# Both attentions of the first block: probabilities as the moving operand, division by the sums moved to GpSimd

## The chip, the cores and the metric

The kernel runs on one core of one Trainium2 chip. The metric is the device time of one execution in microseconds (us), the median of three runs. TensorE is called PE, VectorE DVE, ScalarE ACT, GpSimd POOL.

## The reference, cut to what matters

The program is two transformer blocks. The change lies in the first, which has two layers (`l` = 0, 1) over 256 positions of width 1024. Each layer has a mixer with two self attentions of 8 query heads (2 key and value heads of 64), then a cross attention of 4 heads of 128 to a memory of 256 rows:

```python
p = jax.nn.softmax(jnp.concatenate([s, sink_l], axis=-1), axis=-1)[..., :-1]   # window attention
o = jnp.einsum('bnkgqs,bnskd->bnqkgd', p.astype(v.dtype), vw)
p = jax.nn.softmax(s, axis=-1)                                                 # dense attention
return jnp.einsum('bkgqs,bskd->bqkgd', p.astype(v.dtype), v)
s = jnp.einsum('bqhd,bmhd->bhqm', q, k).astype(jnp.float32) / math.sqrt(X_HEAD_DIM)
p = jax.nn.softmax(s, axis=-1)                                                 # cross attention
o = jnp.einsum('bhqm,bmhd->bqhd', p.astype(v.dtype), v)
return o.reshape(B, S, X_WIDTH) @ wo
```

The division by the softmax sums can be done on the probabilities or on the output; the result is the same.

## The kernel before, in words

**Weights.** Every large product is done as three products of rounded halves. A weight arrives by DMA in pieces of up to 128x1024 elements (`raw`), ACT rounds it (`wh`, L1047), and DVE subtracts to get the rest (`lows`, L1579, two SBUF inputs). PE then runs `three`: high by high, high by low, low by high (L492, in the helper `run`). `lows_for` and `highs_of` look ahead by `LA = 3` pieces: when DVE comes to item n of its program, it makes the low part of piece n + 3.

**Self attention.** The 16 heads are worked on in 8 units of 4 heads and 128 queries (`unit(un)`; `hold` is the place of the unit in S and PT, which alternates). Between the steps of the units stand the `fills`, which are products that don't depend on them: 24 gate products (one 128x1024 piece each), then 24 branch products (`merge`, 128x512 each). Iteration `un` on PE is: the scores of unit `un` (L704), the transposes of the exponentials of unit `un - 1` (`probs_turned`, in L602), three fills, `finish(un - 1)`: the product with the values (L683), one more fill, and the transposes of the output (`oT`, in L602). After iteration 7 the transposes and `finish` of unit 7 follow. There are two layers, so 16 units. DVE takes the maxima of a unit, waits for ACT's exponentials (`sums`), takes the reciprocal of the sums (L1816), makes the lows of the fills, multiplies the product with the values by that reciprocal (`o`, L1841), and after ACT has copied the high half of the transposed output (`oh`, L1179) takes the low half (`ol`, L1845). In the merge fills DVE also has a multiply by the gate for each (`mul`, L1768).

**Cross attention.** Scores (L760); exponentials; the value projection `mv` of four pieces; 16 transposes of the exponentials (L602); 16 products with the values (L778); `xo` on DVE (L1919), 8 transposes of the output, the halves `xoh` (L1249) and `xol` (L1924), and the output projection `wo`, whose four pieces each need their low part (L1579).

**PSUM banks.** The small products rotate over the four banks of `A`. `A.take(w, name, *until)` takes the next bank and waits for the `until` of what was in it four takes before. Each engine's order is that of the program text; each `w.wait_ge` blocks all that stands behind it on that engine.

## Time and profile before

| | before |
|---|---|
| median of 3 runs | 1575.55 us (1572.67 to 1577.36) |
| the profiled execution, its own time | 1578.58 us |
| its span from first to last instruction | 1576.8 us |
| PE busy | 1527.9 us (97%) |
| DVE busy | 1034.4 us (66%) |
| ACT busy | 792.9 us (50%) |
| POOL busy | 228.5 us (14%) |

The span is 1.8 us less than the execution's own time. A busy PE is not a PE at its peak, since matmul records overlap; what a group of matmuls costs is the distance from its first start to the start of what follows. An fp32 matmul stands in the records twice, an fp32 transpose once.

### The profile page before, as it was taken

To read this page: it belongs to the slowest core of one execution; us is meant where nothing else is said; L and a number is where in the kernel's file an instruction comes from. 1 tells how busy PE (TensorE), PEld (TensorE's weight loads), DVE (VectorE), ACT (ScalarE), POOL (GpSimd) and SP (SyncE) were. 2 spreads that over 40 slices of the span, in tenths; PEclk is the share of its full clock that TensorE was granted. 3 is DMA by queue.
4 is the path that set the end of the run, shared out by engine and by line. 5 is a ranking of instruction groups with operands and counts; after the bars stand their busy time and mean duration, and the time that the engine had idled before them with its cause. 6 is when DMAs were issued, how large, how long until landed. Compare 5 with 4: busy or idle time off the path is not lost.

```text
span 1576.8 us, 24954 instructions
## 1 busy us (share of the span) xinstructions
PE 1527.9 (97%) x10255; PEld 1378.4 (87%) x10255; DVE 1034.4 (66%) x1704; ACT 792.9 (50%) x1373; POOL 228.5 (14%) x190
## 2 busy tenths in 40 slices
PE   9999999899999999999999999999999999999999
PEld 6899989799987889988879998687998899989887
DVE  5765586778856585468578874746584687666743
ACT  5554453466643446444546663344445764455532
POOL 2300032121101130021121110103010132100000
PEclk9989999999999999999999999999998999999999
DMA  8623255355565534245444555555311344645453
GB/s 315 244 97 109 92 209 194 117 203 180 183 218 176 198 116 152 70 138 201 181 160 166 185 198 187 192 187 204 118 58 62 108 147 146 209 165 183 169 191 121
DMA packets 40353, 258.19 MB, mean 164 GB/s; under 512 B 4512, under 2 KB 5168, under 8 KB 14000
## 3 DMA queue, kind: packets, MB, share of 16 engines
q1 hardware_dynamic: 35600, 238.44, 43.4%
q0 software_dynamic: 2272, 12.57, 2.2%
q10 hardware_dynamic: 2368, 5.58, 0.9%
q8 instruction: 81, 1.33, 0.3%
q14 instruction: 32, 0.26, 0.1%
HBM read 254.98 MB, written 1.07 MB: 162 GB/s over the span
## 4 chain that ended last, share of the span: by engine, by line
PE 79%; DVE 11%; ACT 6%; DMA 2%; issue 1%; POOL 1%; ACTq 0%; POOLq 0%; DVEq 0%; SPq 0%
PE ps L492 68%; DVE lows L1579 5%; PE ps L602 4%; ACT wh L1047 3%; PE ps L683 2%; PE ps L968 1%; DMA raw<-d_wst 1%; PE ps L704 1%; PE ps L981 1%; ACT arR L1560 1%; DVE S L2306 1%; DVE xTr L1598 1%; PE ps L722 1%; PE ps L778 0%; PE ps L721 0%
## 5 line engine op out<-in xcount | busy, mean ns | idle before, releaser
L1579 DVE TENSOR_TENSOR lows<-raw,wh 128x1024 fp32r<-128x1024 f32 (+3 forms) x473 | 545.0, 1171 | 249.0 <-ACT wh L1047 246.4
L492 PE MATMUL ps<-xTr,wh 128*128 128x256 f32 (+2 forms) x3472 | 635.5, 285 | 6.7 <-DVE lows L1579 4.6
L492 PEld LDWEIGHTS ps<-xTr,wh 128*128 128x128 f32 (+2 forms) x3472 | 539.5, 191 | 11.7 <-ACT arR L1498 3.6
L1047 ACT CAST wh<-raw 128x1024 fp32r<-128x1024 f32 (+3 forms) x473 | 455.0, 989 | 170.4 <-DMA raw<-d_wst 127.8
L492 PE MATMUL ps<-xTr,lows 128*128 128x256 f32 (+1 forms) x1736 | 492.1, 283 | 0.0
L492 PEld LDWEIGHTS ps<-xTr,lows 128*128 128x128 f32 (+1 forms) x1736 | 330.9, 191 | 0.0
L492 PE MATMUL ps<-wh,arR 128*128 128x512 f32 x928 | 297.9, 398 | 7.4 <-DVE ar L1768 4.0
L492 PEld LDWEIGHTS ps<-wh,arR 128*128 128x128 f32 x928 | 175.2, 189 | 52.3 <-DVE ar L1768 5.7
L492 PE MATMUL ps<-lows,arR 128*128 128x512 f32 x464 | 183.9, 396 | 0.0
L492 PE MATMUL ps<-wh,xTr 128*128 128x512 f32 x480 | 152.5, 395 | 16.2 <-DVE xTr L1598 13.2
L492 PE MATMUL ps<-arR,wh 128*128 128x256 f32 (+1 forms) x832 | 148.0, 280 | 0.3
L492 PEld LDWEIGHTS ps<-arR,wh 128*128 128x128 f32 (+1 forms) x832 | 126.7, 188 | 1.1 <-issue 0.8
L492 PEld LDWEIGHTS ps<-wh,xTr 128*128 128x128 f32 x480 | 90.8, 189 | 39.0 <-DVE xTr L1598 15.2
L492 PE MATMUL ps<-arR,lows 128*128 128x256 f32 (+1 forms) x416 | 115.9, 279 | 0.0
L492 PEld LDWEIGHTS ps<-lows,arR 128*128 128x128 f32 x464 | 87.7, 189 | 20.0
L2323 POOL TENSOR_TENSOR sm<-sm,cst 128x1 f32<-128x1 f32 (+3 forms) x27 | 43.2, 1602 | 392.5 <-DVE sm L1618 255.5
L492 PE MATMUL ps<-lows,xTr 128*128 128x512 f32 x240 | 94.0, 392 | 0.0
L492 PEld LDWEIGHTS ps<-arR,lows 128*128 128x128 f32 (+1 forms) x416 | 78.1, 188 | 0.0
L1294 ACT ACTIVATE S<-ps,ar 128x256 f32<-128x256 f32 x88 | 48.6, 561 | 46.1 <-PE ps L492 46.0
L2387 POOL TENSOR_TENSOR ar<-ar 128x256 f32<-128x256 f32 x32 | 31.9, 997 | 233.8 <-DVE ar L1768 233.8
L2399 POOL TENSOR_TENSOR S<-S 128x256 f32<-128x256 f32 x44 | 34.3, 779 | 208.4 <-ACT S L1273 208.4
L492 PEld LDWEIGHTS ps<-lows,xTr 128*128 128x128 f32 x240 | 45.5, 190 | 9.1
(259 smaller groups left out, 1501.7 us busy)
## 6 DMA issues: line engine op xcount, KB each, us to landing
raw<-d_wst SPq DMA_DIRECT2D x196, 1024.0 KB, 4.8
raw<-d_wst SPq DMA_DIRECT2D x24, 512.0 KB, 3.5
raw<-d_wst SPq DMA_DIRECT2D x12, 896.0 KB, 4.5
raw<-d_wst SPq DMA_DIRECT2D x8, 672.0 KB, 4.6
ar<-d_lnp POOLq DMA_DIRECT2D x5, 1024.0 KB, 5.1
raw<-d_wst SPq DMA_DIRECT2D x8, 441.0 KB, 3.4
ar<-d_par POOLq DMA_DIRECT2D x2, 1192.0 KB, 9.6
ar<-d_scr POOLq DMA_DIRECT2D x1, 2048.0 KB, 8.6
```

The source lines that it names most:

```text
L492: op = e.matmul(out, s, m, start=start and i == 0, stop=stop and i == len(pairs) - 1)
L602: op = e.transpose(o, x, ident[0:x.shape[0], 0:x.shape[0]])
L683: op = e.matmul(b[:, h * 64:(h + 1) * 64], PTv[:, hold + h, k, :], va[:, k, v:v + 64], start=(k == 0), stop=(k == 1))
L704: op = e.matmul(bv[:, k, :], qT[br][lo:lo + 64, 2 * hh + k, i * 128:(i + 1) * 128], kT[br][lo:lo + 64, :], start=True, stop=True)
L722: op = e.matmul(bv[:, gg, :], ones[:, 0:128], bs[:, gg * 128:(gg + 1) * 128], start=False, stop=True)
L968: op = e.matmul(b[:, h * 65:(h + 1) * 65], PTv[:, hold + h, k, :], vb[:, k, 4 * br + h, :], start=(k == 0), stop=(k == nkt - 1))
L1047: e.copy(high_of(m), raw_of(m)).then_inc(*high.done(m))
L1294: e.activation(hc[:, s, :], M["up", l, m][:, 0:T], ACT.Identity, bias=cb[:, m:m + 1], scale=ck[:, m, 1:2]).then_inc(*act.done("h", l, m))
L1579: e.tensor_tensor(low_of(m), raw_of(m), high_of(m).bitcast(F32), ALU.subtract).then_inc(*low.done(m))
L2323: return e.tensor_tensor(dst, src, mhalf[0:p, 0:n], ALU.pow)
L2387: e.tensor_tensor(merged[:, d, :], merged[:, d, :], gates[:, gate_at[n] + d, :], ALU.add).then_inc(*pool.done("merged", l, n, d))
L2399: e.tensor_tensor(hc[:, s, :], hc[:, s, :], hc[:, s + 1, :], ALU.mult).then_inc(*pool.done("z", l, n))
```

## The change

In both attentions the operands of the product with the values change places. The values become the stationary operand and the transposed probabilities move, so that the output comes out transposed and the output's transposes on PE, their banks and the buffers `osb`, `xo` go. In the self attention two heads that share their values are now one matmul of 64 output rows and 256 columns, and the two value heads write the rows 0 to 63 and 64 to 127 of one bank. A multiply by the reciprocal on the output is no longer possible in this form, so POOL scales the exponentials in place, 128x1024 elements a unit, between `sums` and the transposes. ACT and DVE take the halves straight from the product's bank, which is given back at `ol`.

```diff
                 def probs_turned(un):
                     hold = unit(un)[3]
-                    w.wait_ge(act, "exp", l, un, 3)
+                    w.wait_ge(pool, "probs", l, un)
...
                 def finish(un):
                     br, i, hh, hold = unit(un)
-                    b = A.take(w, ("pv", l, un), vec, "o", l, un)
+                    b = A.take(w, ("pv", l, un), vec, "ol", l, un)
+                    bv = b[:, 0:256].rearrange("p (h q) -> p h q", q=128)
...
-                    for h in range(4):
-                        v = 128 * br + (h % 2) * 64
-                        for k in range(2):
-                            op = e.matmul(b[:, h * 64:(h + 1) * 64], PTv[:, hold + h, k, :], va[:, k, v:v + 64],
+                    for k in range(2):
+                        for g in range(2):
+                            v = 128 * br + g * 64
+                            op = e.matmul(bv[64 * g:64 * g + 64, :, :], va[:, k, v:v + 64], PTv[:, hold + g:hold + g + 3:2, k, :],
                                           start=(k == 0), stop=(k == 1))
                     op.then_inc(*cross.done("pv", l, un))
                     fill_next(1)
-                    b = A.take(w, ("oT", l, un), vec, "ol", l, un)
-                    bv = b[:, 0:256].rearrange("p (k t) -> p k t", t=128)
-                    w.wait_ge(vec, "o", l, un)
-                    turned(("oT", l, un), [bv[:, k, :] for k in range(2)],
-                           [osb[:, 64 * hold + k * 128:64 * hold + (k + 1) * 128] for k in range(2)])
...
-                    w.wait_ge(act, "xexp", l, i, 3)
+                    w.wait_ge(pool, "xprobs", l, i)
...
-                            op = e.matmul(b[:, h * 128:(h + 1) * 128], PTv[:, 4 * i + h, k, :], Vx[:, k, h * 128:(h + 1) * 128],
+                            op = e.matmul(b[:, h * 128:(h + 1) * 128], Vx[:, k, h * 128:(h + 1) * 128], PTv[:, 4 * i + h, k, :],
...
-                for i in range(2):
-                    b = A.take(w, ("xoT", l, i), vec, "xol", l, i)
-                    bv = b[:, :].rearrange("p (k t) -> p k t", t=128)
-                    w.wait_ge(vec, "xo", l, i)
-                    turned(("xoT", l, i), [bv[:, k, :] for k in range(4)], [xo[i][:, k * 128:(k + 1) * 128] for k in range(4)])
...
-                    w.wait_ge(cross, "pv", l, un)
-                    w.wait_ge(vec, "ri", l, un)
...
-                    e.tensor_tensor(osb[:, 64 * hold:64 * hold + 256].rearrange("p (h d) -> p h d", d=64),
-                                    A["pv", l, un][:, 0:256].rearrange("p (h d) -> p h d", d=64),
-                                    ri.unsqueeze(2).to_broadcast([128, 4, 64]), ALU.mult).then_inc(*vec.done("o", l, un))
...
+                def probs_scaled(un):
+
+                    hold = unit(un)[3]
+                    ri = smalls(96 + 48 * (un % 2))[3]
+                    w.wait_ge(vec, "ri", l, un)
+                    e.tensor_tensor(Sv[:, hold:hold + 4, :], Sv[:, hold:hold + 4, :], ri.unsqueeze(2).to_broadcast([128, 4, T]),
+                                    ALU.mult).then_inc(*pool.done("probs", l, un))
+
+                probs_scaled(0)
                 w.wait_ge(vec, "qg", l, 1)
                 rope_sin(1, 1)
+                for un in range(1, 8):
+                    probs_scaled(un)
...
+                for i in range(2):
+                    ri = smalls(96 + 48 * i)[3]
+                    w.wait_ge(vec, "xri", l, i)
+                    e.tensor_tensor(Sv[:, 4 * i:4 * i + 4, :], Sv[:, 4 * i:4 * i + 4, :], ri.unsqueeze(2).to_broadcast([128, 4, T]),
+                                    ALU.mult).then_inc(*pool.done("xprobs", l, i))
```

Three places in the engines' queues. First PE, at the end of iteration 1 of layer 0: the output's transposes (`ps<-cst,ar`), the scores of unit 2 (`ps<-ar`), and the transposes of unit 1's exponentials (`ps<-cst,S`). Before:

```order
L602 MATMUL ps<-cst,ar 128x128 [waits s_vec]
L602 MATMUL ps<-cst,ar 128x128
L704 MATMUL ps<-ar 128x256 x4
L602 MATMUL ps<-cst,S 128x128 [waits s_act]
L602 MATMUL ps<-cst,S 128x128 x3
L602 MATMUL ps<-cst,S 128x128 [waits s_vec]
L602 MATMUL ps<-cst,S 128x128 x3
```

And of the changed kernel:

```order
L699 MATMUL ps<-ar 128x256 [waits s_vec]
L699 MATMUL ps<-ar 128x256 x3
L601 MATMUL ps<-cst,S 128x128 [waits s_pool]
L601 MATMUL ps<-cst,S 128x128 x3
L601 MATMUL ps<-cst,S 128x128 [waits s_vec]
L601 MATMUL ps<-cst,S 128x128 x3
```

The two transposes with their wait for DVE are gone, and the first group of transposes of the exponentials waits for POOL where it waited for ACT. The second group waits for DVE in both: it takes the bank that `ol` of the unit before gives back.

Second DVE, in iteration 1: the reciprocal, the four lows of the fills, `o` and `ol`, and the copy of the transposed exponentials. Before:

```order
L1816 RECIPROCAL sm<-sm 128x4 [waits s_vec]
L1579 TENSOR_TENSOR lows<-raw,wh 128x1024 [waits s_high] x4
L1841 TENSOR_TENSOR ar<-ps,sm 128x256 [waits s_cross]
L1845 TENSOR_TENSOR arR<-ps,arR 128x2x128 [waits s_act]
L1827 COPY PT<-ps 128x512 [waits s_cross]
```

And of the changed kernel:

```order
L1806 RECIPROCAL sm<-sm 128x4 [waits s_vec]
L1569 TENSOR_TENSOR lows<-raw,wh 128x1024 [waits s_high] x4
L1825 TENSOR_TENSOR arR<-ps,arR 128x2x128 [waits s_act]
L1817 COPY PT<-ps 128x512 [waits s_cross]
L1782 ISA S,sm<-ps,cst 128x256
```

Only `o` is gone; the four lows still follow the reciprocal that POOL's new operation waits for.

Third POOL in layer 0. Before:

```order
L2380 TENSOR_TENSOR ar<-ar 128x512 [waits s_pool]
L2357 TENSOR_TENSOR ar<-ar,cst 128x10x32 [waits s_vec]
L2387 TENSOR_TENSOR ar<-ar 128x256 [waits s_vec] x8
L2387 TENSOR_TENSOR ar<-ar 128x256 [waits s_pool,s_vec] x8
L2323 TENSOR_TENSOR sm<-sm,cst 128x1 [waits s_vec] x2
```

And of the changed kernel:

```order
L2353 TENSOR_TENSOR ar<-ar 128x512 [waits s_pool]
L2360 TENSOR_TENSOR S<-S,sm 128x1024 [waits s_vec]
L2330 TENSOR_TENSOR ar<-ar,cst 128x10x32 [waits s_vec]
L2360 TENSOR_TENSOR S<-S,sm 128x1024 [waits s_vec] x7
L2372 TENSOR_TENSOR ar<-ar 128x256 [waits s_vec] x8
L2372 TENSOR_TENSOR ar<-ar 128x256 [waits s_pool,s_vec] x8
```

Eight operations of 128x1024 stand among the rest, one for each unit; two more follow for the cross attention, so 20 in both layers.

## Rows read from the trace of the kernel before

**Rows 1.** Windows, two stretches of layer 0: start:end, length, PE, PEld, DVE, ACT, POOL busy (x)

```profile
72.00:168.00 96.00, 96.00 (x740) 90.24 (x740) 55.59 (x112) 50.69 (x112) 5.78 (x4) 0.95 0.30 105
168.00:202.00 34.00, 30.72 (x258) 29.10 (x257) 19.30 (x41) 14.86 (x39) 1.84 (x2) 1.00 0.29 94
```

**Rows 2.** Waits of PE: in total, times, longest

```profile
PE ps L602 <- DVE ar L1841: 6.6, 6, 1.5
```

**Rows 3.** Timeline, iteration 1 of layer 0: start, length, engine, line, count, [idle before]

```profile
98.07 0.18 DVE L1816 RECIPROCAL sm<-sm 128x4 f32<-128x4 f32 x1
98.74 5.14 DVE L1579 TENSOR_TENSOR lows<-raw,wh 128x1024 fp32r<-128x1024 f32 x4 [0.49 <-ACT wh L1047]
99.57 1.90 PE L683 MATMUL ps<-ar,PT 128*128 128x64 f32 x16
104.71 1.14 PE L704 MATMUL ps<-ar 64*128 64x256 f32 x8
```

**Rows 4.** Timeline, iteration 3 of layer 0

```profile
128.71 3.84 DVE L1579 TENSOR_TENSOR lows<-raw,wh 128x1024 fp32r<-128x1024 f32 x3 [0.49 <-ACT wh L1047]
...
132.05 1.90 PE L683 MATMUL ps<-ar,PT 128*128 128x64 f32 x16
```

**Rows 5.** Timeline, PE, a product of 60 stationary columns

```profile
1077.70 5.58 PE L492 MATMUL ps<-raw,S 128*60 128x256 f32 x25 [1.17 <-DVE S L2048]
```

**Rows 6.** Timeline, iterations 6 and 7 of layer 0

```profile
175.01 0.69 DVE L1579 TENSOR_TENSOR lows<-raw,wh 128x512 fp32r<-128x512 f32 x1 [0.33 <-ACT wh L1047]
...
179.31 0.42 DVE L1768 SCALAR_TENSOR_TENSOR ar<-ar,ps 128x256 f32<-128x256 f32 x1 [0.86 <-PE ps L492]
...
180.22 0.41 PE L602 MATMUL ps<-cst,ar 128*128 128x128 f32 x2 [0.94 <-DVE ar L1841]
...
181.63 1.09 PE L602 MATMUL ps<-cst,S 128*128 128x128 f32 x8
...
186.85 0.18 DVE L1816 RECIPROCAL sm<-sm 128x4 f32<-128x4 f32 x1 [2.00 <-ACT S L1154]
187.35 0.69 DVE L1579 TENSOR_TENSOR lows<-raw,wh 128x512 fp32r<-128x512 f32 x1 [0.33 <-ACT wh L1047]
...
190.76 0.41 DVE L1768 SCALAR_TENSOR_TENSOR ar<-ar,ps 128x256 f32<-128x256 f32 x1
...
191.66 0.41 PE L602 MATMUL ps<-cst,ar 128*128 128x128 f32 x2 [1.50 <-DVE ar L1841]
191.90 1.04 PE L602 MATMUL ps<-cst,S 128*128 128x128 f32 x8
```

**Rows 7.** Timeline, operations of POOL of three sizes

```profile
329.01 0.73 POOL L2399 TENSOR_TENSOR S<-S 128x256 f32<-128x256 f32 x1 [9.43 <-ACT S L1273]
...
75.04 1.30 POOL L2380 TENSOR_TENSOR ar<-ar 128x512 f32<-128x512 f32 x1
...
254.59 2.78 POOL L2334 TENSOR_SCALAR xs<-xs 128x1024 f32<-128x1024 f32 x1 [1.49 <-PE ps L602]
```

**Rows 8.** Timeline, an operation of POOL and one of DVE together

```profile
219.02 0.86 POOL L2387 TENSOR_TENSOR ar<-ar 128x256 f32<-128x256 f32 x1 [1.49 <-DVE ar L1768]
...
219.20 1.76 DVE L1579 TENSOR_TENSOR lows<-raw,wh 128x1024 fp32r<-128x1024 f32 x1
```

**Rows 9.** Timeline, cross attention of layer 0

```profile
275.66 0.17 DVE L1905 TENSOR_SCALAR sm<-sm 128x4 f32<-128x4 f32 x1
...
277.83 0.18 DVE L1907 RECIPROCAL sm<-sm 128x4 f32<-128x4 f32 x1 [2.00 <-ACT S L1235]
...
278.77 4.63 DVE L1579 TENSOR_TENSOR lows<-raw,wh 128x1024 fp32r<-128x1024 f32 x4 [0.76 <-ACT wh L1047]
...
289.66 0.60 PE L602 MATMUL ps<-cst,ar 128*128 128x128 f32 x4
...
291.75 0.47 PE L492 MATMUL ps<-wh,arR 128*128 128x512 f32 x1 [0.49 <-DVE arR L1924]
...
292.86 2.36 DVE L1579 TENSOR_TENSOR lows<-raw,wh 128x1024 fp32r<-128x1024 f32 x2 [0.26 <-ACT wh L1047]
```

More of the change, by code:

```diff
@@ L341, in build @@
         osb = arena(512)
-        xo = [osb, ar[:, gates_o:gates_o + 512]]
         mb = ar[:, 0:1024].rearrange("p (i c) -> p i c", i=2)
@@ L770, in tensor @@
                 for i in range(2):
-                    b = A.take(w, ("xpv", l, i), vec, "xo", l, i)
+                    b = A.take(w, ("xpv", l, i), vec, "xol", l, i)
                     w.wait_ge(act, "xpT", l, i, 0)
@@ L1175, in finish @@
                     fill_next(1)
-                    w.wait_ge(cross, "oT", l, un)
+                    w.wait_ge(cross, "pv", l, un)
                     if br:
@@ L1179, in finish @@
                     e.copy(outT[br].h[:, 2 * hh:2 * hh + 2, i * 128:(i + 1) * 128],
-                           A["oT", l, un][:, 0:256].rearrange("p (k t) -> p k t", t=128)).then_inc(*act.done("oh", l, un))
+                           A["pv", l, un][:, 0:256].rearrange("p (k t) -> p k t", t=128)).then_inc(*act.done("oh", l, un))
                 for un in range(8):
@@ L1247, in scalar @@
                 for i in range(2):
-                    w.wait_ge(cross, "xoT", l, i)
-                    e.copy(oxT.h[:, :, i * 128:(i + 1) * 128], A["xoT", l, i][:, :].rearrange("p (k t) -> p k t", t=128)
+                    w.wait_ge(cross, "xpv", l, i)
+                    e.copy(oxT.h[:, :, i * 128:(i + 1) * 128], A["xpv", l, i][:, :].rearrange("p (k t) -> p k t", t=128)
                            ).then_inc(*act.done("xoh", l, i))
@@ L1831, in finish @@
                     br, i, hh, hold = unit(un)
-                    ri = smalls(96 + 48 * (un % 2))[3]
                     c = slice(i * 128, (i + 1) * 128)
                     fill_next(1)
-                    w.wait_ge(cross, "pv", l, un)
-                    w.wait_ge(vec, "ri", l, un)
-                    if un > 1:
-                        w.wait_ge(cross, "oT", l, un - 2)
-                    elif l:
-                        w.wait_ge(cross, "xoT", l - 1, 1)
-                    e.tensor_tensor(osb[:, 64 * hold:64 * hold + 256].rearrange("p (h d) -> p h d", d=64),
-                                    A["pv", l, un][:, 0:256].rearrange("p (h d) -> p h d", d=64),
-                                    ri.unsqueeze(2).to_broadcast([128, 4, 64]), ALU.mult).then_inc(*vec.done("o", l, un))
                     w.wait_ge(act, "oh", l, un)
-                    e.tensor_tensor(outT[br].l[:, 2 * hh:2 * hh + 2, c], A["oT", l, un][:, 0:256].rearrange("p (k t) -> p k t", t=128),
+                    e.tensor_tensor(outT[br].l[:, 2 * hh:2 * hh + 2, c], A["pv", l, un][:, 0:256].rearrange("p (k t) -> p k t", t=128),
                                     outT[br].h[:, 2 * hh:2 * hh + 2, c].bitcast(F32), ALU.subtract).then_inc(*vec.done("ol", l, un))
@@ L1914, in vector @@
                 for i in range(2):
-                    ri = smalls(96 + 48 * i)[3]
-                    w.wait_ge(cross, "xpv", l, i)
-                    w.wait_ge(vec, "xri", l, i)
-                    w.wait_ge(cross, "oT", l, 7)
-                    e.tensor_tensor(xo[i].rearrange("p (h d) -> p h d", d=128), A["xpv", l, i][:, :].rearrange("p (h d) -> p h d", d=128),
-                                    ri.unsqueeze(2).to_broadcast([128, 4, 128]), ALU.mult).then_inc(*vec.done("xo", l, i))
-                for i in range(2):
                     c = slice(i * 128, (i + 1) * 128)
                     w.wait_ge(act, "xoh", l, i)
-                    e.tensor_tensor(oxT.l[:, :, c], A["xoT", l, i][:, :].rearrange("p (k t) -> p k t", t=128), oxT.h[:, :, c].bitcast(F32),
+                    e.tensor_tensor(oxT.l[:, :, c], A["xpv", l, i][:, :].rearrange("p (k t) -> p k t", t=128), oxT.h[:, :, c].bitcast(F32),
                                     ALU.subtract).then_inc(*vec.done("xol", l, i))
```

## The prediction

> **What bounds the kernel now.** PE is busy for 97% of the span, so I read the windows of the first layer first: from 72 to 168 us, which holds most of the units, PE has records in all 96.00 us while DVE is busy for 55.59; from 168 to 202, the iterations 6 and 7 and the end of unit 7, PE lacks 3.3 us of 34 and DVE is busy for 19.3 [rows 1]. PE's waits name that lack: 6.6 us in six waits, three a layer, for `o` (L1841) before the output's transposes [rows 2]. So a cycle taken off PE in the attention counts, unless another engine's chain becomes the last to end. The timelines of iteration 1, of iterations 6 and 7 and of the cross attention show how near these chains are.
>
> **What goes from PE.** The product with the values starts at 99.57 with 16 records over 1.90 us; less the length of a single record, 0.28, that is 15 steps of 0.108, so 1.70 us to the next start [rows 3]. The two transposes of the output take two steps of 0.11, 0.22 us.
>
> **What comes to PE.** Four matmuls of 64 stationary columns and 256 moving ones, 8 records. No pair of matmuls that write different output rows stands in the trace, so I take two bounds. Alone, a record with 60 stationary columns takes (5.58 - 0.38)/24 = 0.217 us [rows 5]: 8 of them are 1.74 us, and with 0.16 for entering and leaving the smaller mode some 1.90, 0.20 more than before. (The 0.16 is an estimate: the scores' 1.14 us [rows 3] are 0.11 more than three steps of 0.217 and one record's 0.38, and I add half of that for the way back.) Side by side, the scores (64 contracted rows, two halves of the array, also 8 records of 256 columns) take 1.14 us from first start to last end [rows 3], which is four steps of 0.21 and not eight. With the switch that is 1.15 us, 0.55 less than 1.70. I take the second, since the two value heads alternate in the program and have no output row in common. The Trainium skill, "TensorEngine Tiling (Array Packing)", section "Key Properties", says that tiles load and multiply independently, in parallel, and that a change of mode drains the engine; by that page too the sum would be the 1.15. The trace agrees for halves by rows, and shows nothing for halves by columns. So a unit gives 0.55 + 0.22 = 0.77 us where PE alone is the bound. The cross attention has as many products of the same size as before.
>
> **What comes to POOL, and what it does to DVE.** 128x256 takes 0.73 us and 128x512 takes 1.30 [rows 7]: 0.57 per 256 elements, so 128x1024 takes 1.30 + 2 x 0.57 = 2.43 us. Upper bound by the nearest row of that size: 2.78 (a TENSOR_SCALAR) [rows 7]. The Trainium skill, "GPSIMD Engine Reference", section "Elementwise — side-by-side cycle accounting", has 4497 ns for a fp32 tensor_tensor of 2048; half of it, an estimate from that page, would be 2.25 us.
>
> The 20 operations, 49 us, lie beside PE's work; but not beside all of DVE's. POOL's 128x256 ran from 219.02 to 219.88; a low part that DVE began at 219.20 took 1.76 us [rows 8] where one normally takes 1.22 (four in 5.14, with small gaps [rows 3]). It ended at 220.96, so its work began at 219.74: DVE stood still until 0.14 us before POOL's end. That is the rule against this change. The Trainium skill states it in "GPSIMD Engine Reference", section "Specifications": the SBUF interfaces are shared with VectorE, with contention when a DVE instruction has two SBUF inputs. By this rule the lows wait; the trace agrees, with the 0.54 us above.
>
> POOL will start 0.08 us after each reciprocal. The next thing on DVE is a low part, 0.33 us after the reciprocal in iterations 6 and 7 and 0.49 in iteration 1 [rows 3, 6]: POOL is first each time, and the low is held for some 2 us.
>
> **Iteration 1.** Reciprocal until 98.25, POOL 98.33 to 100.76, the first low done at 100.62 + 1.22 = 101.85 and not at 99.96 [rows 3]. It belongs to the fourth fill (three ahead), which began at 99.57 + 1.70 = 101.27 and could now begin at 100.7. It begins at 101.9. With no transposes behind it the scores start at 104.86 where they started at 104.71 [rows 3]: 0.15 lost, and the 0.77 with it.
>
> **Iterations 2 to 5.** The same 2 us of delay meet a first low that is done at 128.71 + 1.22 = 129.93 in iteration 3, when the fourth fill begins after 132.05 + 1.70 = 133.75 [rows 4]: 3.8 us ahead, so nothing waits. 4 x 0.77 = 3.1 gained.
>
> **Iterations 6 and 7.** The fills are half as long and each adds a `mul` to DVE. The second half of the transposes of the exponentials takes the bank of the previous unit's product, so it waits for `ol`, which stands behind lows and `mul`s. In iteration 6 the first low starts at 177.06 for 175.01 [rows 6], 2.05 late; 0.19 and 0.86 of idle time before the second low and the third `mul` (179.31) absorb 1.05. The `mul` ends near 180.55 and `ol` takes `o`'s place: 180.9. The second transposes start at 180.95 and not at 181.63 + 0.44 = 182.07, a gain of 1.1. In iteration 7 all of DVE's chain is 1.1 earlier and then held by 2.05: `ol`, in the place of `o` at 190.76 + 0.33 = 191.09 [rows 6], starts at 191.09 - 1.14 + 2.05 = 192.0 and ends at 192.4. The second transposes start at 192.5, where they started at 191.90 + 0.44 = 192.34 [rows 6]: 0.15 lost over both, though the waits of 0.94 and 1.50 [rows 6] are gone. What is late next is the transposes of unit 7, and behind them two fills.
>
> **After unit 7.** The product 0.55, the transposes 0.22, and the third wait, 3.3 - 0.94 - 1.50 = 0.86 plus 0.15 of start: 1.8 gained.
>
> A layer's self attention gives -0.15 + 3.1 - 0.15 + 1.8 = 4.6 us, both 9.2.
>
> **Cross attention.** `wo` would start at 289.76 and not at 291.75 [rows 9]: 2.0 less. Two things give it back. POOL's first operation starts near 274.5 and holds the small DVE operation at 275.66 (if that one needs the shared interface; no row has such a small one inside an operation of POOL) until 276.8, 1.15 late; then the second reciprocal ends at 279.15 and not at 278.01, POOL runs to 281.7, and the low of the fourth `mv` piece, begun at 278.77 [rows 9], ends at 282.75. PE wants it near 281.2: 1.5 lost, or 0.5 if the small operation is not held. And the low of the fourth `wo` piece (292.86 [rows 9]) stands behind ACT's second copy; it moves by less than PE: 0.7 lost. I take 2.0 - 1.5 - 0.7 = about 0, with 0.8 a layer as the better end.
>
> **Sum.** 9.2 us off the profiled execution's 1578.58 is 1569.4. That execution lies 3.0 above the median of the runs, so against the median I say 1575.55 - 9.2 = 1566.4. Some 0.3%, 4.7 us, is what a measurement can tell here from no change.
>
> **The rivals.**
>
> - **The halves don't run side by side.** Then a product costs 0.2 more than before where I have 0.55 less. Iterations 1, 6 and 7 end the same, since DVE ends them; iterations 2 to 5 give 4 x 0.02 and unit 7's end 1.05. A layer gives 0.8 to 1.0: 1573.7. For it: only row halves are shown, in two banks, and here both write one bank. 0.15.
> - **POOL holds up nobody.** The wait of DVE would have to be shorter for this operation than in rows 8. Then iteration 1 gains 0.9 (0.77 and the small start of the wait), 2 to 5 3.1, 6 and 7 2.8 with DVE's own chain of lows and `mul`s as the limit, unit 7 1.8, the cross attention 1.3: 9.9 a layer, 1555.8. Against it: DVE waits out POOL in every such pair that I looked at. 0.15.
> - **POOL's operation takes longer.** Each microsecond of it costs 1 in iteration 1, 2 in iterations 6 and 7, and up to 2 in the cross attention: 5 a layer, 10 in both. At 2.78 the gain is 5.7, at 2.9 to 3.3 it is 4.5 to 0.5, about 1573.5 with the other small losses. 0.10.
> - **Slower.** The same mechanism with POOL losing the start: if a low is first, POOL waits its 1.22 us out and holds the next one, 2.43 + 1.22 = 3.65, or 4.0 with the 2.78. By 10 us for each microsecond that is 1575.55 - 9.2 + 12.2 = 1578.6 to 1582. It decides against the change from 3.35 us on, and by more than 0.3% from 3.8. For it: the margin of the start is 0.25 us in the late units. Against it: DVE waits there for ACT's rounding, which the change leaves alone. 0.10.
>
> The forecast itself has 0.50, between 1562 and 1571. **Numbers.** Faster by over 0.3% (below 1570.8): the forecast but for 0.04 of it, and the second rival, 0.61. Slower (above 1580.3): 0.08. The rest, 0.31, is within. The range reaches from the second rival to the near end of the last: 1556 to 1577.
>
> **What would show it.** PE: the new product's 8 records within 1.1 us (1.9 would be the first rival); no output transposes. POOL: ten operations a layer of 2.4 us, each starting 0.1 after a reciprocal. DVE: the first low after each reciprocal some 2 us longer or later than 1.22. PE's waits: for `lows` of 0.7 to 1.2 us at iteration 1 and in iterations 6 and 7, for `ol` before the second transposes there, none for `o`; in the cross attention a wait of 0.5 to 1.5 for the last `mv` low. The prediction is wrong if these waits are missing (faster) or if POOL's operations take 3.3 or more (no gain or a loss).

## The result

The changed kernel takes 1558.89 us (median of 4 runs, 1558.53 to 1559.93) where the kernel before takes 1576.45 beside it: a ratio of 0.9883, 95% interval 0.9861 to 0.9905. That is inside the range and on the side that was forecast. But the gain is 17.6 us where 9.2 were worked out, so the sum is off by almost half, and the time lies outside the 1562 to 1571 to which the forecast itself gave its 0.50. All ratios here and below go by executions in the fast state; one of `g_outer`, 2447.37 us at a granted clock of 0.554, is left out of them.

The page of the changed kernel, the execution of 1559.93 us:

```profile
span 1558.1 us, 24610 instructions
PE 1511.7 (97%) x10079; PEld 1353.0 (87%) x10079; DVE 1046.8 (67%) x1684; ACT 793.1 (51%) x1373; POOL 266.4 (17%) x210
```

PE is still the bound. Its waits (us in total, times, longest) have changed their cause: none is for `o` any more [rows 2], and those for lows (7.7 us, seven times, in the kernel before) have grown. The longest, 3.4 us, is outside the attentions and the same in both kernels:

```profile
PE ps L491 <- DVE lows L1569: 13.8, 17, 3.4
```

**What POOL does to DVE.** The timeline of iteration 1 (start, length; it answers to [rows 3]), iteration 7 (to [rows 6]) and the cross attention (to [rows 9]):

```profile
97.60 0.18 DVE L1806 RECIPROCAL sm<-sm 128x4 f32<-128x4 f32 x1
97.86 1.89 POOL L2360 TENSOR_TENSOR S<-S,sm 128x1024 f32<-128x1024 f32 x1 [6.35 <-DVE sm L1806]
98.27 2.56 DVE L1569 TENSOR_TENSOR lows<-raw,wh 128x1024 fp32r<-128x1024 f32 x1 [0.49 <-ACT wh L1037]
...
181.48 1.89 POOL L2360 TENSOR_TENSOR S<-S,sm 128x1024 f32<-128x1024 f32 x1 [8.77 <-DVE sm L1806]
...
181.74 2.19 DVE L1569 TENSOR_TENSOR lows<-raw,wh 128x512 fp32r<-128x512 f32 x1 [0.33 <-ACT wh L1037]
...
183.98 0.50 PE L491 MATMUL ps<-arR,wh 128*128 128x256 f32 x2 [1.62 <-DVE lows L1569]
...
266.73 1.89 POOL L2380 TENSOR_TENSOR S<-S,sm 128x1024 f32<-128x1024 f32 x1 [13.96 <-DVE sm L1887]
...
267.86 0.80 DVE L1885 TENSOR_SCALAR sm<-sm 128x4 f32<-128x4 f32 x1
```

The low that began at 98.27 ended at 100.83, 1.08 behind POOL's end at 99.75. A low takes 1.22, so its work began 0.14 before that end, as in [rows 8]. All 14 lows of 128x1024 elements behind a division end 1.08 after POOL; the four of 128x512 (0.69 us by themselves) end 0.55 after it. The small TENSOR_SCALAR of the cross attention takes 0.80 for its 0.17 and ends with POOL. So the hold is real. Its size is not the one forecast: POOL's operation takes 1.89 us, in all twenty, and not 2.43. PE's wait in iteration 7, 1.62, is its largest for a low in the attentions.

**What PE gets.** The product of unit 1, and PE's groups at the ends of the stages, first of the kernel after:

```profile
115.23 1.08 PE L683 MATMUL ps<-PT,ar 128*64 128x256 f32 x8
116.24 0.51 PE L491 MATMUL ps<-xTr,wh 128*128 128x256 f32 x2
...
164.27 0.49 PE L699 MATMUL ps<-ar 64*128 64x256 f32 x2
174.92 1.14 PE L699 MATMUL ps<-ar 64*128 64x256 f32 x8
175.99 1.11 PE L601 MATMUL ps<-cst,S 128*128 128x128 f32 x8
...
185.50 1.03 PE L601 MATMUL ps<-cst,S 128*128 128x128 f32 x8
244.78 0.38 PE L601 MATMUL ps<-cst,xs 128*128 128x128 f32 x2
293.94 0.38 PE L601 MATMUL ps<-cst,xs 128*128 128x128 f32 x2
```

and three that [rows 3, 6] lack, of the kernel before:

```profile
168.22 0.49 PE L704 MATMUL ps<-ar 64*128 64x256 f32 x2
252.59 0.38 PE L602 MATMUL ps<-cst,xs 128*128 128x128 f32 x2
302.65 0.38 PE L602 MATMUL ps<-cst,xs 128*128 128x128 f32 x2
```

The product takes 1.01 us from its start to the next group's, where it took 1.70. The lead over the kernel before, by stage of layer 0: 104.71 - 103.95 = 0.76 at the end of iteration 1, 3.95 at the end of iteration 5 (168.22 - 164.27), 6.40 before the transposes of unit 7 (191.90 - 185.50), 7.81 ahead of the cross attention, 8.71 behind it (by the starts of the transposes of x). In layer 1 the cross attention gives the same 0.90.

### The profile page after: what moved, and what is told of

Read it like the earlier page. It is cut to its first block, busy times and chain, and to the rows that moved or that the text cites. A ratio compares the mean times of both kernels' runs of the same rounds, so it can differ in the third digit from the quotient of the medians.

```text
span 1558.1 us, 24610 instructions
## 1 busy us (share of the span) xinstructions
PE 1511.7 (97%) x10079; PEld 1353.0 (87%) x10079; DVE 1046.8 (67%) x1684; ACT 793.1 (51%) x1373; POOL 266.4 (17%) x210
## 3 DMA queue, kind: packets, MB, share of 16 engines
q8 instruction: 80, 1.31, 0.3%
## 4 chain that ended last, share of the span: by engine, by line
PE 78%; DVE 11%; ACT 6%; DMA 2%; issue 1%; POOL 1%; ACTq 0%; POOLq 0%; DVEq 0%; SPq 0%
PE ps L491 69%; DVE lows L1569 5%; PE ps L601 3%; ACT wh L1037 3%; PE ps L958 1%; DMA raw<-d_wst 1%; PE ps L971 1%; PE ps L699 1%; ACT arR L1550 1%; ACT S L1144 1%; DVE S L2279 1%; DVE xTr L1588 1%; PE ps L683 1%; PE ps L717 1%; PE ps L773 0%
## 5 line engine op out<-in xcount | busy, mean ns | idle before, releaser
L1569 DVE TENSOR_TENSOR lows<-raw,wh 128x1024 fp32r<-128x1024 f32 (+3 forms) x473 | 566.6, 1221 | 239.4 <-ACT wh L1037 238.9
L2360 POOL TENSOR_TENSOR S<-S,sm 128x1024 f32<-128x1024 f32 x16 | 30.3, 1893 | 160.4 <-DVE sm L1806 160.4
```

What stands on the lines that cost most here:

```text
L1569: e.tensor_tensor(low_of(m), raw_of(m), high_of(m).bitcast(F32), ALU.subtract).then_inc(*low.done(m))
L2360: e.tensor_tensor(Sv[:, hold:hold + 4, :], Sv[:, hold:hold + 4, :], ri.unsqueeze(2).to_broadcast([128, 4, T]), ALU.mult).then_inc(*pool.do ...
```

## The experiments

All ratios are to the kernel before, whose runs stand beside each on its chip. An execution also has stretches in which PE's granted clock falls to the lower level; over the runs the mean is 0.984 to 0.993, and an estimate, 0.001 of a span of 1558 us, puts 1.6 us on each 0.001 of it. So spans of single executions differ by some microseconds, and I read the medians or ratios and, apart from them, PE's waits. In two executions of the changed kernel (`after` and `after_again`) the waits for lows in both attentions together are 7.6 and 8.4 us, so less than 1 us of difference in them says nothing.

### Two ways of leaving or keeping the division

The division left out (`noscale`):

```
-                    w.wait_ge(pool, "probs", l, un)
+                    w.wait_ge(act, "exp", l, un, 3)
...
-                    e.tensor_tensor(Sv[:, hold:hold + 4, :], ... ALU.mult).then_inc(*pool.done("probs", l, un))
```

> The division is left out: the transposes take the exponentials as they are and wait for ACT, as in the kernel before, and the output is not normalised; the product and all else is the changed kernel. Theory (POOL's hold of DVE): the waits of PE for lows that the changed kernel's trace shows in a layer (0.31, 0.16, 1.62, 0.28 and 0.78 us) go or shrink to what ACT alone sets, at most 3.1 a layer, 6.3 in both: 1552.6 to 1555 us, and the lows after each reciprocal take 1.22 and 0.69 us. Rival (POOL holds up nobody): 1559. If PE's cycles alone made the whole gain, this run is also 1559.

Measured: 1555.85 us, ratio 0.985 (0.9832 to 0.9867). The low behind unit 1's reciprocal is back at 1.22 and the wait of iteration 7 at 0.28:

```profile
98.15 2.54 DVE L1569 TENSOR_TENSOR lows<-raw,wh 128x1024 fp32r<-128x1024 f32 x2 [0.49 <-ACT wh L1037]
...
181.90 0.50 PE L491 MATMUL ps<-arR,wh 128*128 128x256 f32 x2 [0.28 <-DVE lows L1569]
```

So the hold is there and costs little: PE's waits for lows in the attentions (60 to 290 and 550 to 780 us) are 3.8 and 3.8 in the changed kernel, 1.6 and 1.7 here. That is 4.3 us (5.1 by the second execution; the two ratios differ by 0.0033, 5 us) for 1.89 us of POOL, not the 19 that 10 us for each would be.

The second operand a dense tile. First the exponentials themselves (`dense`), then a tile of constants (`dense2`):

```
-   Sv[:, hold:hold + 4, :], ri.unsqueeze(2).to_broadcast([128, 4, T]),
+   Sv[:, hold:hold + 4, :], Sv[:, hold:hold + 4, :],                      (dense)
+   S[..].rearrange("p (a c) -> p a c", c=512), C[:, 0:512].unsqueeze(1).to_broadcast([128, 2, 512]),   (dense2)
```

> The division's second operand is a dense 128x1024 tile (the exponentials themselves) and not the four reciprocals broadcast along each row, so the output holds squares in place of quotients; all else is the changed kernel. Theory (the record's: DVE stands still while POOL works, 10 us of time for each microsecond of POOL's operation): if the size rule of rows 7 holds for two dense operands, the operation takes 2.43 us and not 1.89, each held low ends 1.08 us behind POOL's end as before, and the time is 1558.9 + 0.54 x 10 = 1564.3 us, with the wait of PE in iteration 7 at 1.6 + 1.1 = 2.7. Rival (POOL's length reaches nobody; the extra gain came from elsewhere): about 1559. Rival on the duration (the broadcast has nothing to do with it): the operation takes 1.89 here too, and the time is about 1559.

> The run with the exponentials as both operands left open whether two different dense tiles cost more: here the second operand is a dense tile of constants of 512 columns, used twice, so the output holds wrong products; all else is the changed kernel. Theory A (rows 7's step of 0.57 us per 256 elements belongs to two different dense operands): the operation takes 2.4 us. Theory B (the length has nothing to do with the operand): 1.89. The time: by the record's price of 10 us per microsecond 1558.9 + 5.4 = 1564.3; by the price that leaving the division out and the extra operation gave (2.3 us a layer for 1.9 us, and some 1 to 2 a layer for 1.0), +1.3 to +2 us, 1560 to 1561. By theory B 1559.

Measured: `dense` 1561.26, ratio 0.9889 (0.9871 to 0.9908), no change that can be told; `dense2` 1566.25, 0.9932 (0.9915 to 0.995). The operation in the one, and in the other:

```profile
125.93 1.90 POOL L2360 TENSOR_TENSOR S<-S 128x1024 f32<-128x1024 f32 x1 [13.47 <-DVE sm L1806]
```

```profile
110.41 2.42 POOL L2360 TENSOR_TENSOR S<-S,cst 128x1024 f32<-128x1024 f32 x1 [11.63 <-DVE sm L1806]
...
181.02 2.36 POOL L2360 TENSOR_TENSOR S<-S,cst 128x1024 f32<-128x1024 f32 x1 [8.78 <-DVE sm L1806]
...
183.98 0.50 PE L491 MATMUL ps<-arR,wh 128*128 128x256 f32 x2 [2.09 <-DVE lows L1569]
...
275.00 0.50 PE L491 MATMUL ps<-wh,arR 128*128 128x512 f32 x1 [1.31 <-DVE lows L1569]
```

What counts is two different dense tiles, not density. With those the operation takes 2.36 to 2.42 us, near the forecast's 2.43, and the kernel is 7.4 us slower than the changed one by the medians; the ratios' intervals leave 3 to 12. The waits for lows give 4 to 5 (6.1 and 6.5 us in the two attentions where it was 3.8 and 3.8, or 4.5 and 3.9). So `dense2` has the length of POOL's operation that the forecast worked with. For the half microsecond upward from 1.89 the waits grow by 8 to 10 us for each microsecond, as the record says; all of it taken away gave 2.3 to 2.7 for each. The trace shows why: at 1.89 us PE's waits in iteration 6 and for the `mv` low are down to 0.16 and 0.28 us, where `dense2` has 0.66 and 1.31, so below 1.89 only iteration 7 has much left to give.

### A second operation on POOL, behind and ahead

```
+   e.tensor_tensor(osb..., osb..., ri[:, 0:2].unsqueeze(2).to_broadcast([128, 2, T]), ALU.mult).then_inc(*pool.done("extra", l, un))
```

behind the division's signal (`extra_after`) or ahead of the division (`extra_before`). The tile is `osb`, which the changed kernel still has for the first products of its program; only the attention no longer uses it.

> A second POOL operation of 128x512 with a broadcast operand, on a tile that nobody reads, stands behind each of the 16 divisions of the self attention, after their signal: it lengthens POOL's hold and delays no transposes. An estimate of its length, half of 1.89 and a little: 1.0 us. Theory (hold): DVE's first low after each reciprocal ends 1.0 later, which costs 1 in iteration 1 and 2 in the iterations 6 and 7: 3 a layer, 6 in both, 1565 us; the wait of PE in iteration 7 grows from 1.6 to 3.6. Rival (what counts of POOL's length is the time until the transposes may start): 1559.

> The same extra operation ahead of each of the 16 divisions, so that both the hold of DVE and the time until the transposes may start grow by 1.0 us. Theory (hold alone): the same 1565 us as with the operation behind. Rival (latency to the transposes): 1565 here and 1559 with the operation behind. If both count, this run is slower than that one by over 1 us.

Measured: 1564.02, ratio 0.9905 (0.9889 to 0.992), and 1559.12, 0.9877 (0.9856 to 0.9898). POOL and DVE, behind and ahead:

```profile
97.43 1.90 POOL L2360 TENSOR_TENSOR S<-S,sm 128x1024 f32<-128x1024 f32 x1 [6.35 <-DVE sm L1806]
99.28 2.02 POOL L2364 TENSOR_TENSOR ar<-ar,sm 128x512 f32<-128x512 f32 x1
...
97.84 6.81 DVE L1569 TENSOR_TENSOR lows<-raw,wh 128x1024 fp32r<-128x1024 f32 x4 [0.49 <-ACT wh L1037]
```

```profile
98.59 1.04 POOL L2362 TENSOR_TENSOR ar<-ar,sm 128x512 f32<-128x512 f32 x1 [6.35 <-DVE sm L1806]
99.59 2.88 POOL L2364 TENSOR_TENSOR S<-S,sm 128x1024 f32<-128x1024 f32 x1
...
178.04 0.66 PE L601 MATMUL ps<-cst,S 128*128 128x128 f32 x4 [0.87 <-DVE arR L1825]
```

Two things are seen. The two engines take turns: when POOL's first operation ends, the waiting low goes first and POOL's second waits 0.98 us for it (2.02 for 1.04, 2.88 for 1.89). So in `extra_after` the first low is held no longer than before. PE's wait in iteration 7 stays at 1.63, where the theory had 3.6, and only a wait of 0.64 for `ol` comes on top in each layer: 1.5 to 2.3 us more in all these waits. Its ratio is 3.5 us above the changed kernel's, with an interval that reaches from nothing to the theory's 6, so the medians alone can't settle that price.

And `extra_before` comes close to the record's slower case, POOL losing the start, in all 16 units: the division itself stands behind a low. It did not cost the 12.2 us that the record's sum has for that case: the ratio is that of the changed kernel, and the interval leaves out the theory's 6. The first low is then held by 1.04 only, and the lateness falls on the transposes, which had room. What it adds is a wait for `ol` (L1825) of 0.65 and of 0.87 in each layer. By PE's starts, from the scores of unit 2 to the transposes of unit 7, it gives 4.6 us a layer over the kernel before where the changed kernel gives 5.7.

### The product's order, and both groups on the same rows

`g_outer` swaps the two loops; `same_half` does that too, and writes both groups to one half of the output rows:

```
-                    for k in range(2):
-                        for g in range(2):
+                    for g in range(2):
+                        for k in range(2):
...
-                            op = e.matmul(bv[64 * g:64 * g + 64, :, :], va...
+                            op = e.matmul(bv[0:64, g, :, :], va...          (same_half only)
```

> The four matmuls of the self attention's product in the order head group outside, keys' half inside, so that only the second and the third write different output rows. Theory (the halves run side by side only when neighbours in the program write different rows): the 8 records take 1.6 to 1.9 us where they take 1.08, so a unit costs 0.5 to 0.8 us more in the iterations that PE ends (0, 2 to 5 and the last, 6 a layer): 6 to 10 us, 1565 to 1569. Rival (the gain of the product comes from the number of records alone, 8 for 16, whatever their order): 1.08 us and 1559.

> The run with the other order left the product at 1.02 us, so the order doesn't say what the side-by-side work is worth. Here both head groups write the same 64 output rows (other columns of the bank), in that same order; the second group's rows are then missing from the output, and what the bank held before stands in their place. Instructions, sizes and waits are those of the run with the other order. Theory (two matmuls overlap because they use different halves of the array's output rows): the 8 records now take 8 x 0.215, about 1.75 to 1.9 us, each unit 0.8 us more; in the iterations that PE ends (0, 2 to 5 and the last, 6 a layer) that is 0.85 each, and a little where lows were waited for: 10 us, 1568 to 1570. Rival (64 stationary columns or 8 records alone make it short): 1.02 us and 1559.

Measured: 1560.8 (1559.4 without the one of 2447.37), ratio 0.9887 (0.9866 to 0.9908), and 1571.56, 0.9969 (0.9957 to 0.998).

```profile
115.75 1.09 PE L683 MATMUL ps<-PT,ar 128*64 128x256 f32 x8
116.77 0.39 PE L491 MATMUL ps<-xTr,wh 128*128 128x256 f32 x1
```

```profile
132.08 1.94 PE L683 MATMUL ps<-PT,ar 128*64 128x256 f32 x8
133.95 0.38 PE L491 MATMUL ps<-xTr,wh 128*128 128x256 f32 x1
```

My theory on the order fell: with one group wholly behind the other the product still takes 1.02 us. What matters is which output rows they have, 1.87 us if they are the same, 0.85 more a unit. The two ratios differ by 0.0082, 13 us, of the 18 that the change gives. The waits for lows are smaller in `same_half` (2.5 and 1.8 us for 4.3 and 4.8): PE comes to them later.

### Only the self attention

The diff of the cross attention is taken back (product with the probabilities stationary, `xo` on DVE, the transposes), the rest stays.

> Only the self attention is changed; the cross attention is that of the kernel before (division on DVE behind the product, the output's transposes, no POOL operation). By PE's starts in the two traces the changed cross attention moved the start of the transposes of x behind it by 0.9 us more than those ahead of it, so the theory is that this part is worth 0.9 a layer, 1.8 in both, against the record's term of 0: 0.989 to 0.990 of the kernel before, 1561, with PE's waits of 0.35 and 0.49 us for the division and the low part back, and those of 0.28 for the mv low and 0.78 for the wo low smaller or gone. Rival (the record's term: the cross attention gives nothing): the time of the changed kernel, and its PE idles as long there. By waits alone the two differ by little more than 1 us; the starts of PE's groups are what tells.

Measured: 1563.08, ratio 0.9909 (0.9894 to 0.9925). PE's start of the transposes of x ahead of the cross attention and behind it, and the two waits of the old form:

```profile
245.45 0.38 PE L602 MATMUL ps<-cst,xs 128*128 128x128 f32 x2
...
283.48 0.65 PE L602 MATMUL ps<-cst,ar 128*128 128x128 f32 x4 [0.35 <-DVE ar L1905]
284.63 0.47 PE L492 MATMUL ps<-wh,arR 128*128 128x512 f32 x1 [0.49 <-DVE arR L1910]
295.53 0.27 PE L602 MATMUL ps<-cst,xs 128*128 128x128 f32 x1
```

50.08 us for the stage, where the changed kernel takes 49.16 and the kernel before 50.06. So the cross attention gives 0.9 a layer. The two ratios (0.9909 and the changed kernel's 0.9883) are too near to show it by themselves.

### Two versions that try to do better

`early_half` divides heads 0 and 1 while ACT still takes the exponentials of heads 2 and 3; `act_scale` divides on ACT; `mixed` takes the early halves, in the cross attention too, and ACT for unit 7 alone.

```
+                    for n in range(2):
+                        two = slice(2 * n, 2 * n + 2)
+                        w.wait_ge(act, "exp", l, un, 2 * n + 1)
+                        e.reciprocal(ri[:, two], su[:, two]).then_inc(*vec.done("ri", l, un, n))
...
+                        e.activation(Sv[:, hold + h, :], Sv[:, hold + h, :], ACT.Copy, scale=ri[:, h:h + 1])    (ACT)
```

> The division moves from POOL to ACT, four activations of 128x256 with the reciprocal as scale, behind the first high part of the next fills (in the cross attention straight behind the exponentials). POOL does none of it. Theory (POOL's hold of DVE is what is left to gain): the lows after each reciprocal take 1.22 and 0.69 us, the wait of PE in iteration 7 falls from 1.6 to 0.3, and the time is that of the run without division, 1555 to 1557. Rival (ACT's high parts come later by its four operations, some 1.4 us an estimate from the exponentials' rows, and DVE's lows with them, so the wait only changes its cause): 1558 to 1561, with a wait of 1 us and more in iteration 7 still, for lows whose releaser is ACT.

> The self attention's division in two halves of two heads: reciprocal and POOL's operation of 128x512 for heads 0 and 1 while ACT still takes the exponentials of heads 2 and 3 (the sink's exponential goes first on ACT). Each half is 1.04 us on POOL. Theory (the hold that counts is what POOL still works after the last reciprocal): it falls from 1.89 to about 1.05; the wait of PE in iteration 7 from 1.6 to 0.8, the 0.31 and 0.16 of the iterations 1 and 6 go: 1.3 a layer, 2.6 in both, 1556. Rival (the small operations of DVE for the second half stand still until POOL's first half ends, as the small one in the cross attention did, 0.80 us for 0.17): POOL's second half starts late, and nothing is gained: 1558 to 1560.

> A version to beat the changed kernel: the division in two early halves on POOL for the units 0 to 6 and for both tiles of the cross attention, and on ACT, behind the first high part, for unit 7, where PE's wait for lows was 1.6 us with POOL, 1.0 with the halves and 0.13 with ACT. Theory (these waits are all that the hold costs): the wait of iteration 7 at some 0.2 and the one for the mv low (0.28) gone: against the changed kernel 1.4 + 0.16 + 0.28, 1.8 to 2.4 a layer, 4 to 5 in both: 1554 to 1555. Rival (what is gained in the attention is waited away again in the stages behind, as the run without the division lost 2 us of its lead behind the cross attention): 1556 to 1559.

> The changed kernel again, beside the two others on one chip, so that their ratios can be read against its own: 0.988 of the kernel before, by every theory.

Measured: `act_scale` 1560.42, 0.9894 (0.9874 to 0.9913); `early_half` 1558.64, 0.9889 (0.9871 to 0.9907); `mixed` 1556.09, 0.9865 (0.9847 to 0.9883); the changed kernel again 1560.0, 0.9896 (0.9873 to 0.9919). The wait of iteration 7 in `early_half`, the wait for `ol` that `act_scale` has for it, and iteration 7 in `mixed`:

```profile
183.16 0.50 PE L491 MATMUL ps<-arR,wh 128*128 128x256 f32 x2 [1.00 <-DVE lows L1569]
```

```profile
177.21 0.66 PE L601 MATMUL ps<-cst,S 128*128 128x128 f32 x4 [0.39 <-DVE arR L1839]
```

```profile
181.36 0.50 PE L491 MATMUL ps<-arR,wh 128*128 128x256 f32 x2 [0.28 <-DVE lows L1579]
```

In `act_scale` ACT needs 1.71 us for its four operations. Of the theory the sign came true and the time did not: PE's wait in iteration 7 is 0.13. Of the rival it is the other way round: the time is in its range, but its wait of 1 us and more in iteration 7 is not there. What came instead are waits for `ol` (0.9 and 1.4 us in the two attentions), since DVE's lows now stand behind ACT's later high parts (DVE idles 1.77 us for one ahead of 173.93), and a cross attention that gives 0.41 and not 0.90 a layer by PE's starts. `early_half` takes away part of what it should: the wait of iteration 7 is 1.00 where 0.8 was expected, waits for lows are 2.9 and 3.3 for 3.8 and 3.8, and those 1.4 us are below what its runs can tell. `mixed` has 2.7 and 2.3, and both signs of its theory, though its time is 1 us above it. Its four runs (1553.63 to 1556.23) all lie under the changed kernel's beside them (1558.8 to 1563.02), though the two ratios' intervals overlap: about 3 to 4 us better, not firmly.

## Why the prediction was right, and where it was wrong

**In the range, and by no more than that.** The mechanism held in its main parts, the shorter product and POOL's hold of DVE. But two terms had errors, both to the same side, and the time is inside the stated range only since that range reached down to the rival without any hold, 1555.8.

**The product and the transposes: right.** 0.77 us a unit forecast; the product went from 1.70 to 1.01, the lead grew from 0.76 to 3.95 us in iterations 2 to 5, so 0.80 a unit, 3.2 for the 3.1. (Of the 0.69 some 0.09 goes again just ahead of the product, which starts 0.21 us after the last record of the fill, 99.49 - 99.28, where the fill's own records follow in 0.12. Record by record the product costs 1.10, and 1.15 was forecast.) The first rival (halves not side by side, 1573.7) is what `same_half` is, but for the length of POOL's operation: 1571.56.

**POOL's operation: the term that was mis-sized.** "128x1024 takes 1.30 + 2 x 0.57 = 2.43 us" goes by operations with two different dense operands [rows 7]. With four reciprocals broadcast it takes 1.89, with two different tiles 2.36 to 2.42. Half of the error of some 8 us comes from here: by `dense2` 4 to 5 us in waits, 7.4 by the medians, and by the record's own price 0.54 x 10 = 5.4.

Stage by stage, with `dense2` in place of the forecast's POOL (when its PE started the scores of unit 6, the transposes of unit 7, and those of x ahead of the cross attention and behind it):

```profile
163.30 0.49 PE L699 MATMUL ps<-ar 64*128 64x256 f32 x2
185.50 0.27 PE L601 MATMUL ps<-cst,S 128*128 128x128 f32 x1
244.80 0.27 PE L601 MATMUL ps<-cst,xs 128*128 128x128 f32 x1
295.01 0.27 PE L601 MATMUL ps<-cst,xs 128*128 128x128 f32 x1
```

- Cross attention: forecast 0, with 1.5 lost for the low of the fourth `mv` piece behind a held small operation. With 2.4 us it gives 7.64 - 7.79 = -0.15 (2.0 - 1.5 - 0.7 is -0.2), and the waits are 1.31 for the 1.5 and 0.79 for the 0.7. The mechanism and the sum hold; at 1.89 the wait is 0.28 and the stage gives 0.90, which `self_only` shows too.
- Iterations 6 and 7: forecast -0.15. At 2.4 us they give 6.40 - 4.92 = 1.48, at 1.89 2.45. So 0.97 is POOL's length, and 1.6 a layer is another error. It is all in iteration 7: up to the scores of unit 7 `dense2` gives 1.19 where 1.1 was forecast for iteration 6, and in iteration 7 0.30 where 1.25 were to be lost.

**Iteration 7: the step that failed.** "The second transposes start at 192.5", because they take the bank that `ol` of the unit before gives back. In the trace after, the eight transposes of unit 7 run without a break from 185.50, the second four from 185.93, while that `ol` begins only at 186.97 and ends at 187.39. Had they needed its bank, they would have stood for 1.46 us. The `ol` of unit 5 and that of unit 6:

```profile
175.98 0.41 DVE L1825 TENSOR_TENSOR arR<-ps,arR 128x256 fp32r<-128x256 f32 x1
...
186.97 0.42 DVE L1825 TENSOR_TENSOR arR<-ps,arR 128x256 fp32r<-128x256 f32 x1
```

The four banks go round. Without `oT` an iteration takes five and not six: scores, scores, transposes, transposes, product. But behind iteration 7 no scores come. Counting four back from the second transposes of unit 7 comes to the first transposes of unit 6, free for long; in the kernel before, with its `oT`, the same count comes to the second transposes of unit 6. Only the transposes within an iteration meet a product's bank. In iteration 7 the second transposes, those of unit 6, take the bank of unit 5's product. They start at 176.49 with that `ol` done at 176.39, and in `extra_before`, where they do wait for it, they start 0.06 after it (178.04 and 177.98). So hardly any room is left there, and in `extra_after`, `extra_before` and `act_scale` this is the wait for `ol` that appears. What ends iteration 7 is the low of the fourth fill, which the record's sum has only in iteration 1 (its list of signs names such a wait, of 0.7 to 1.2, for iteration 7 too; it was 1.62).

**Iteration 1 and the end.** From the product of unit 0 (99.57 and 99.49) to the scores of unit 2, iteration 1 gave 0.68 where -0.15 was forecast (from its own start of the fill, 101.9, the scores come at 104.96 and not at 104.86, since fill and switch take 3.06: 103.95 - 100.89). But this stage is not the same in two executions of the same kernel: PE's wait there was 0.31 and 0.36 in the two layers of the one, 1.05 and 0.42 in the other, whose first layer gave -0.06. So what came over the forecast here has no cause that the runs show; `dense2` with 0.37 and -0.11 lies among them. Behind unit 7 1.4 came for 1.8.

Layer 0 by these stages: 0.76 + 3.19 + 2.45 + 1.41 + 0.90 = 8.7 for 4.6. Layer 1 starts with 1.6 us more lead, from a stretch of lower clock in the one execution (granted 0.83 from 510 to 520 us in the kernel before, 1.00 in that after), and gets 1.5 more behind unit 7 in the same way (granted 0.84 from 720 to 730 us). Neither is a gain of the change.

**Where luck comes in.** `dense2` takes 1566.25 and the forecast was 1566.4. By PE's starts `dense2` gives 12.2 us from the first product on, not 9.2, since the 1.6 a layer of iteration 7 is still missing in the forecast. By its ratio it gives 8 to 13. So that the two times agree to 0.2 us is chance.

**The other rivals.** POOL holds up nobody, 1555.8: DVE is held each time. Without the division the time is 1555.85, but beside a kernel before that was slower on that chip: the ratio is 0.985 (to 0.9867), the rival's was 0.9875. The bound was a little short, and by PE's starts it was so in iterations 6 and 7, 4.2 us a layer where the rival had 2.8 with DVE's chain as the limit. That is the error of iteration 7 again, with no POOL in it. POOL losing the start, 1578.6 to 1582: something close to it made to happen in `extra_before`, 1559.12. Its step "10 us for each microsecond" carried the price of a longer single hold over to a case in which two shorter ones take turns with the low between them.

**What the trace of before had.** I wrote that no row has a small operation of DVE inside one of POOL. There is one, right beside a row that I used [rows 7]:

```profile
75.22 1.14 DVE L1805 TENSOR_TENSOR sm<-ar,sm 128x4 f32<-128x4 f32 x1
```

It is held for the whole of POOL's 75.04 to 76.34. The term was right without it.

**What of the signs.** As forecast: the product's 8 records in 1.08 us, ten POOL operations a layer, none of PE's waits for `o`. Not as forecast: 1.89 us for POOL's 2.4, first lows 1.1 to 1.5 us longer and not some 2, no wait for `ol`, waits for lows of 0.31 to 1.05 in iteration 1, 0.16 in iteration 6, 1.62 in iteration 7, and 0.28 for the last `mv` low where 0.5 to 1.5 was said.

## What to carry to other kernels

Before you extrapolate a duration, look what the operands are: a broadcast column and a second dense tile are not the same price, and the row of the nearest size may be the wrong kind. When a change takes something out of a ring of buffers, count the ring anew for each place, since who waits for whom moves with it. A price for each microsecond of a delay holds only near where it was worked out, and for a delay of the same form: here half a microsecond more in one piece cost 8 to 10 for 1 in PE's waits, one microsecond more with a low between the pieces about 2, and taking all 1.89 away gave 2.3 to 2.7 for each, since of the waits that it feeds those of iteration 6 and of the `mv` low were by then nearly gone.

## What the runs showed of the hardware

- POOL's tensor_tensor, 128 partitions, fp32: 1.04 us for 512 elements and 1.89 for 1024 with a broadcast operand, and 1.90 for 1024 with one tile as both operands; 1.30 [rows 7] and 2.36 to 2.42 with two different dense tiles. The Trainium skill, "GPSIMD Engine Reference", section "Elementwise — side-by-side cycle accounting", has 4497 ns for 2048 elements of a fp32 tensor_tensor, and half of it, an estimate, is 2.25; `dense2` is 5 to 8% above that.
- The hold is by turns, and by whole instructions: a low and POOL's next operation alternate (2.02 for 1.04, 2.88 for 1.89). Of DVE's small operations beside a division, a TENSOR_TENSOR (0.52 us here) and a TENSOR_SCALAR (0.80 for 0.17) on SBUF stand still, a RECIPROCAL (0.17) doesn't. In `early_half`, POOL, and DVE's two:

```profile
97.56 1.04 POOL L2363 TENSOR_TENSOR S<-S,sm 128x512 f32<-128x512 f32 x1 [5.54 <-DVE sm L1807]
...
98.11 0.52 DVE L1805 TENSOR_TENSOR sm<-sm 128x2 f32<-128x2 f32 x1 [0.62 <-ACT S L1148]
...
180.52 2.04 POOL L2363 TENSOR_TENSOR S<-S,sm 128x512 f32<-128x512 f32 x2 [8.39 <-DVE sm L1807]
...
181.18 0.17 DVE L1807 RECIPROCAL sm<-sm 128x2 f32<-128x2 f32 x1 [0.75 <-ACT S L1148]
```

- Not every operation of POOL holds DVE. The one with `pow` on 128x10 elements takes 2.87 us, and a low that begins inside it takes its usual 1.21; the kernel after has the same. No run here shows what makes the difference. POOL and DVE, in the kernel before:

```profile
70.82 2.87 POOL L2323 TENSOR_TENSOR sm<-sm,cst 128x10 f32<-128x10 f32 x1 [0.38 <-DVE sm L1696]
...
71.87 1.21 DVE L1579 TENSOR_TENSOR lows<-raw,wh 128x1024 fp32r<-128x1024 f32 x1
```

- Two column halves of the array work side by side even when all of one group stands ahead of the other in the program: 1.02 us against 1.01, and 1.87 on the same rows. The Trainium skill, "TensorEngine Tiling (Array Packing)", section "Key Properties", has tiles work independently; the trace agrees, for halves by columns now too.
